# Folding a 2048-point token DFT by even and odd parts, and a small product cut into four column strips

## The chip, the cores and the metric

The kernel runs on 1 core of one Trainium2 chip (the chip has 8). The metric is the device time of one execution in microseconds (us). A run with the hardware profiler shows every instruction of every engine: TensorE (PE, with its weight loads as PEld), VectorE (DVE), ScalarE (ACT), GpSimd (POOL) and SyncE, whose queue SPq issues almost all DMAs here.

## The reference

One layer of a hybrid backbone, on 2048 latent and 256 context tokens of width 1024, in fp32. The parts that the change touches:

```python
mod = silu(c) @ w_ada + b_ada                      # 2 vectors (latent, context), 1024 -> 6144: shift, scale, gate, twice
h   = norm(x) * (1 + scale1) + shift1
z   = h @ w_in                                     # za, zb, q, k, v
def fourier(zb, fw):                               # zb: tokens x 4 groups x 64 channels
    zf = fft2(zb, axes=(tokens, channels), norm='ortho').real
    return einsum('blgc,gcd->blgd', zf, fw)
y = concat(gmlp(za), fourier(zb), attend(q, k, v)) @ w_out
x = affine_ln(ALPHA * x + gate1 * y)
...
x = affine_ln(ALPHA * x + gate2 * conv_ffn(...))
```

The 2-D DFT is done as a channel part (64 points, with `f_w` folded in, in the projection phase) and a token part (2048 points for the latents, 256 for the context, in the Fourier phase). Only the real part is kept.

## The kernel before

It is one program of seven phases, one after another, each a block with a barrier at its end: modulation, projection, Fourier, attention, mix (output projection and norm), FFN up, FFN down. The order on each engine is written by hand, and engines meet at semaphores. Products of high precision are made in three passes of fp32r parts (`PASSES`: high-high, high-low, low-high); ACT rounds a tile to its high part, DVE subtracts for the low part.

**Modulation** (`modulation_phase`). `w_ada` is 1024 x 6144. It is multiplied in chunks of 512 columns (`ADA_COLS`), each with 8 products over k: the stationary side is `silu` (128 x 2), the moving side 128 x 512 of the chunk, and the result takes 2 of the 128 PSUM partitions (L154). Four chunks are made here, eight in the Fourier phase (`ada_product`, L945), where PE has them between pieces of the DFT. Two chunk slots in SBUF; SP loads chunk n when chunk n-2 is done. Between the chunks SP loads `w_in` through a ring of six staging pieces (L114), which ACT rounds (L142) and DVE completes (L165).

**Projection** (`projection_phase`). Nine groups of 256 tokens. `every_group` writes out group 0, runs groups 1 to 6 in a hardware loop of two, and writes out 7 and 8. The channel DFT (`channel_dft`) reads `zbt`, a copy of zb with tokens along the free side, and its rows go to the scratch tensor `chan_dft` (2048+256 tokens x 512: real and imaginary parts of two halves), by `store_ab`.

**Fourier** (`fourier_phase`). The 2048 tokens are split as 4 x 512. For each of four slices i, SP loads 1 MB of `chan_dft` (L791); DVE makes a radix-4 butterfly (L873, L881, L887) and multiplies by twiddles (L897 to L902); ACT rounds (L842) and DVE completes (L909). PE then multiplies with a 512-point table (2 MB, loaded once, L793): 192 instructions of 128x128 weights on 512 columns (`terms`, L954). In between it makes an `ada_product`, and for the cached keys four transposes (`turn_past`, L967). ACT copies results out (L854). The context DFT is 32 instructions at the end (L992). On SP each chunk load is followed by its bias and by the store of an earlier chunk's row, which wait for DVE's sum (L866).

**Mix** (`mix_phase`). 18 tiles of 128 tokens: PE turns a tile of y with eight transposes (`turn_y`, L1639), multiplies with `w_out` in 48 instructions (L1648), and turns the normed tile (L1658). Tiles 2 to 11 run in a hardware loop.

## Time and profile before

| | |
|---|---|
| median of 3 runs | 3102.55 us (3098.46 to 3105.24) |
| the profiled execution | 3104.43 us, span 3102.0 us |
| PE busy | 2874.1 us (93%) |
| DVE busy | 1849.3 us (60%) |
| ACT busy | 1279.6 us (41%) |
| POOL busy | 401.6 us (13%) |
| DMA | 429.97 MB, mean 139 GB/s |
| modulation, projection, Fourier | 0 to 65, 65 to 602, 602 to 739 us |
| attention, mix, FFN | 740 to 1250, 1250 to 1520, 1520 to 3102 us |

Busy times are shares of the span, which is the profiled execution from its first to its last instruction; the run's own time is 2.4 us longer. An engine's busy time says little about a single phase: what matters in a phase is which engine or transfer ends last before its barrier.

### The profile page before, as it was taken

How to read it: one execution, taken by the hardware profiler on the slowest of the kernel's cores; microseconds unless marked ns; L12 is line 12 of the kernel's file. 1: busy time of each engine (PE TensorE's matmuls, PEld its weight loads, DVE VectorE, ACT ScalarE, POOL GpSimd, SP SyncE). 2: the span in 40 equal slices, each digit the busy share in tenths (PEclk: the TensorE clock that was granted, in tenths of full speed). 3: DMA queues.
4: the chain of work that ended last, by engine and by line, in shares of the span. 5: the costliest groups of instructions: out<-in, count | busy, mean ns of one | idle time of the engine just before them, and what ended most of it. 6: DMA issues, size and time to landing. Idle time of an engine off the chain costs nothing. (4 is left out here: it accounts for less than half of the span.)

```text
span 3102.0 us, 51048 instructions
## 1 busy us (share of the span) xinstructions
PE 2874.1 (93%) x17132; PEld 2545.3 (82%) x17132; DVE 1849.3 (60%) x3199; ACT 1279.6 (41%) x2746; POOL 401.6 (13%) x567
## 2 busy tenths in 40 slices
PE   3899999797999999799699999999999979999997
PEld 0899999644887888587599999999999978888875
DVE  4443432262998899477788777666766643443545
ACT  3111111112887888133355565555655532121111
POOL 0000000012222222122400000000000000311312
PEclk8899999898999999899799999999999989999998
DMA  7322222367544560545364555454445435243333
GB/s 251 101 82 92 91 75 74 134 246 199 132 102 89 123 141 16 165 162 185 94 224 166 172 180 185 149 162 149 145 150 163 148 132 169 78 136 117 106 127 131
DMA packets 374228, 429.97 MB, mean 139 GB/s; under 512 B 91911, under 2 KB 270486, under 8 KB 371382
## 3 DMA queue, kind: packets, MB, share of 16 engines
q1 hardware_dynamic: 355353, 418.55, 43.5%
q10 hardware_dynamic: 18720, 9.44, 1.0%
q8 instruction: 88, 1.44, 0.2%
q14 instruction: 67, 0.54, 0.1%
HBM read 305.71 MB, written 124.19 MB: 139 GB/s over the span
## 5 line engine op out<-in xcount | busy, mean ns | idle before, releaser
L1978 PE MATMUL fu_alpha<-fu_h,fu_w 128*128 128x384 f32 x3168 | 577.6, 337 | 19.2 <-DVE fu_h L2204 10.6
L1978 PEld LDWEIGHTS fu_alpha<-fu_h,fu_w 128*128 128x128 f32 x3168 | 556.7, 190 | 21.4 <-issue 21.3
L2464 PE MATMUL fd_acc<-fd_w,fd_f 128*128 128x512 f32 x2376 | 546.2, 392 | 26.5 <-DVE fd_w L2492 17.1
L2464 PEld LDWEIGHTS fd_acc<-fd_w,fd_f 128*128 128x128 f32 x2376 | 447.4, 189 | 125.2 <-issue 17.8
L1978 PE MATMUL fu_beta<-fu_h,fu_w 128*128 128x384 f32 x1584 | 285.4, 334 | 1.2 <-DVE fu_h L2204 1.2
L1978 PEld LDWEIGHTS fu_beta<-fu_h,fu_w 128*128 128x128 f32 x1584 | 275.5, 188 | 1.4 <-issue 1.4
L517 PE MATMUL pj_gps<-pj_ht,w_in 128*128 128x256 f32 x2160 | 268.1, 284 | 0.0
L517 PEld LDWEIGHTS pj_gps<-pj_ht,w_in 128*128 128x128 f32 x2160 | 262.7, 192 | 1.3
L2488 DVE TENSOR_TENSOR fd_f<-fd_f_stage,fd_f 128x512 fp32r<-128x512 f32 (+1 forms) x110 | 91.4, 832 | 284.2 <-ACT fd_f L2444 284.2
L2444 ACT CAST fd_f<-fd_f_stage 128x512 fp32r<-128x512 f32 (+1 forms) x110 | 63.4, 579 | 443.9 <-PE fd_acc L2464 389.3
L2178 DVE TENSOR_TENSOR fu_w<-up_w_stage,fu_w 128x512 fp32r<-128x512 f32 x264 | 181.6, 689 | 85.8 <-ACT fu_w L2042 82.7
L507 PE MATMUL pj_gps<-w_in,pj_ht 128*128 128x512 f32 x912 | 215.7, 394 | 5.3 <-DVE pj_ht L599 5.2
L1648 PE MATMUL mx_acc<-out_w,mx_yt 128*128 128x512 f32 x864 | 208.1, 400 | 0.0
L507 PEld LDWEIGHTS pj_gps<-w_in,pj_ht 128*128 128x128 f32 x912 | 171.1, 189 | 40.9 <-DVE pj_ht L599 5.6
L1282 PE MATMUL at_o_ps<-at_v_parts,at_prob_hi 128*128 128x192 bf16 (+1 forms) x1152 | 195.4, 248 | 1.1 <-DVE at_osum L1350 1.1
L1648 PEld LDWEIGHTS mx_acc<-out_w,mx_yt 128*128 128x128 f32 x864 | 162.7, 190 | 38.2
L2042 ACT CAST fu_w<-fu_w_sums 128x512 fp32r<-128x512 f32 x198 | 122.9, 622 | 164.8 <-PE fu_beta L1978 158.5
L2042 ACT CAST fu_w<-up_w_stage 128x512 fp32r<-128x512 f32 x264 | 163.2, 618 | 61.3 <-PE fu_gamma L1978 56.5
L1282 PE MATMUL at_o_ps<-at_v_parts,at_prob_lo 128*128 128x128 bf16 (+1 forms) x1152 | 186.5, 219 | 0.0
L2178 DVE TENSOR_TENSOR fu_w<-fu_w_sums,fu_w 128x512 fp32r<-128x512 f32 x198 | 136.4, 689 | 53.4 <-ACT fu_w L2042 50.3
L2235 DVE SCALAR_TENSOR_TENSOR fu_result<-fu_g,fu_conv_w,fu_result 128x768 f32<-128x768 f32 (+1 forms) x132 | 134.2, 1016 | 47.2 <-ACT fu_result L2082 46.1
L1978 PE MATMUL fu_gamma<-fu_h,fu_w 128*128 128x384 f32 x792 | 148.4, 335 | 0.0
(194 smaller groups left out, 4294.2 us busy)
## 6 DMA issues: line engine op xcount, KB each, us to landing
up_w_stage<-in_w_gu_dram SPq DMA_DIRECT2D x88, 512.0 KB, 4.2
fu_w_sums<-w_gu_sums SPq DMA_DIRECT2D x132, 256.0 KB, 3.3
fd_w_stage<-in_w_down_dram SPq DMA_DIRECT2D x54, 512.0 KB, 3.6
fd_f_stage<-f_t SPq DMA_DIRECT2D x88, 256.0 KB, 2.7
at_k<-k_t SPq DMA_DIRECT2D x28, 704.0 KB, 12.7
w_gu_sums<-fu_w_sums SPq DMA_DIRECT2D x66, 256.0 KB, 4.9
fo_w<-in_w_ada_dram SPq DMA_DIRECT2D x8, 2048.0 KB, 8.8
up_w_stage<-in_w_gu_dram SPq DMA_DIRECT2D x44, 256.0 KB, 4.6
```

Source lines behind the costliest of these rows:

```text
L507: mm = pe.matmul(out, ht[a][:, s, k, t * P:(t + 1) * P], w[b][:, k, col:col + 512], start=(k, a, b) == (0, HI, HI), stop=(k, a, b) == (KT ...
L517: mm = pe.matmul(out[:, m * G_TOK:(m + 1) * G_TOK], w[a][:, k, col + m * P:col + (m + 1) * P], ht[b][:, s, k, :], start=(k, a, b) == (0, H ...
L1282: mm = pe.matmul(o_ps[:, s, 0:width * HD], part[0:rows, s, b, :], vp[0:rows, parity, v, 0:width, :].rearrange("p n d -> p (n d)"), start=i ...
L1648: mm = pe.matmul(acc[:, s, half * 512:(half + 1) * 512], yt[a][:, s, k, :], w[b][:, k, half * 512:(half + 1) * 512], start=(k, a, b) == (0 ...
L1978: mm = pe.matmul(out, w[x][:, j, k, :], b[y][:, j, k, :], start=opens and (k, x, y) == (0, HI, HI), stop=(k, x, y) == (KH - 1, LO, HI), sk ...
L2042: act.copy(w[HI][:, j], w_source(m, par, j)).then_inc(w_hi, 1)
L2178: dve.tensor_tensor(w[LO][:, j], w_source(m, par, j), w[HI][:, j].bitcast(F32), ALU.subtract).then_inc(w_lo, 1)
L2235: dve.scalar_tensor_tensor(out, grow[:, par, tp:tp + n], par1(cw[:, tp], f), out, ALU.mult, ALU.add).then_inc(tap[tp], 1)
L2444: act.copy(f[HI][:, slot, 0:n], fst[:, slot, 0:n]).then_inc(f_hi, 1)
L2464: mm = pe.matmul(acc[:, t, at], f[a][:, slot, t * P:(t + 1) * P], w[b][:, w_at(st, slot), at], start=is_step(st, 0) and (a, b) == (HI, HI) ...
L2488: dve.tensor_tensor(f[LO][:, slot, 0:n], fst[:, slot, 0:n], f[HI][:, slot, 0:n].bitcast(F32), ALU.subtract).then_inc(f_lo, 1)
```

## The change

**The token DFT is folded.** For a 2048-point DFT of which only the real part is kept, tokens t and 2048-t meet the same cosine and opposite sines, and tokens t and 1024-t the same up to the parity of the output. So DVE adds and subtracts four quarters of the tokens (`fold`), and what is left is four products of 512 tokens with four 512x512 tables (cosine and sine, even and odd outputs). To have token t and its mirrors on one partition, quarters 1 and 3 are stored in reversed order by the projection phase: ACT copies `zbt` with columns reversed for these groups, and `store_ab` writes tiles in reversed order. The bounds of `every_group` must then be numbers, and the hardware loop of groups 1 to 6 is written out. Cosine part and sine part go to separate accumulators; their sum is output k, their difference output 2048-k, for k from 0 to 1023. The first goes to `y`, the second to a new scratch tensor `y_rev` in the order of k, so the mix phase has to turn it over: for tiles 8 to 15 it loads 256 of the 1024 columns from `y_rev` and, in place of two of eight transposes, multiplies with an exchange matrix. Single tokens (0, 512 mirrored, 1024) and output 1024 are treated apart (`e512`, `signs`, `mid`).

**The `w_ada` product is cut in strips.** A chunk of 512 columns becomes four strips of 128 columns, whose products go to columns 0, 32, 64 and 96 of the PE array (`tile_position`) and so to four groups of PSUM partitions. The biases are added by four instructions of 2x128 instead of one of 2x512, in both phases. The Fourier phase has three chunk slots; biases are loaded once and rows stored at its end.

**The order in the Fourier phase is new.** All slices of x, then all four tables (4 MB) are loaded, then the chunks. PE starts after all slices are folded, and the last four `ada_product`s come after the context DFT.

```diff
+def ada_chunk_product(pe, acc, silu, w):
+    for k in range(KT):
+        for q in range(ADA_STRIPS):
+            mm = pe.matmul(acc[ada_strip(q), 0:ADA_STRIP], silu[:, k, :], w[:, k, q * ADA_STRIP:(q + 1) * ADA_STRIP],
+                           start=k == 0, stop=k == KT - 1, tile_position=(0, q * (P // ADA_STRIPS)))
+    return mm
...
-            with eng.Fori(0, (GROUPS - 3) // 2) as i:
-                for s in range(2):
-                    body(i * 2 + (1 + s), 1 - s, True, LAT, False)
+            for g in range(GROUPS - 2):
+                body(g, g % 2, True, LAT, False)
...
+                def load_x(i):
+                    t = i * P
+                    p0 = 1 if i == 0 else 0
+                    sp.dma_start(x[:, i, SET_A, :], chan_dft[t:t + P, :]).then_inc(x_loaded[i], 16)
+                    sp.dma_start(x[p0:P, i, SET_C, :], chan_dft[QUARTER - 1 + t + p0:QUARTER - 1 + t + P, :]).then_inc(x_loaded[i], 16)
+                    if i == 0:
+                        sp.dma_start(x[0:1, i, SET_C, :], chan_dft[HALF_T:HALF_T + 1, :]).then_inc(x_loaded[i], 16)
+                    sp.dma_start(x[p0:P, i, PLUS, :], chan_dft[3 * QUARTER - 1 + t + p0:3 * QUARTER - 1 + t + P, :]).then_inc(x_loaded[i], 16)
+                    sp.dma_start(x[p0:P, i, MINUS, :], chan_dft[HALF_T + t + p0:HALF_T + t + P, :]).then_inc(x_loaded[i], 16)
...
+                fold(0)
+                dve.wait_ge(mid_loaded, 32)
+                dve.tensor_tensor(e512[:, :].rearrange("p (h c) -> p h c", h=2), part(ex[:, 0, :], 0), part(ex[:, 1, :], 0), ALU.add)
...
+                for i in range(1, I):
+                    fold(i)
+                    low_folded(i - 1)
+                low_folded(I - 1)
+                for n in range(4):
+                    dve.wait_ge(table_hi, n + 1)
+                    dve.tensor_tensor(table[LO][:, n], table_raw[:, n], table[HI][:, n].bitcast(F32), ALU.subtract).then_inc(table_lo, 1)
...
+                def transform(m):
...
+                    for n, (tab, side, ri, par) in enumerate(TERMS):
+                        if m == 0:
+                            pe.wait_ge(table_lo, tab + 1)
...
+                        for i in range(I):
+                            for a, b in PASSES:
+                                mm = pe.matmul(o, table[a][:, tab, i, m * P:(m + 1) * P], part(f[b][:, i, side - PLUS, :], ri),
...
                     for k in range(KT):
-                        mm = pe.transpose(yps[:, k, :], yb[:, s, k * P:(k + 1) * P], ident[:, :])
+                        at = slice(k * P, (k + 1) * P)
+                        if mirrored(t) and D_A <= k * P < D_A + D_B:
+                            mm = pe.matmul(yps[:, k, :], yb[:, s, at], exchange[:, :], start=True, stop=True)
+                        else:
+                            mm = pe.transpose(yps[:, k, :], yb[:, s, at], ident[:, :])
```

PE, start of the Fourier phase, before (`fo_kps` are the transposes of cached keys):

```order
L945 MATMUL fo_ada_acc<-fo_w,fo_silu 2x512 x8
L954 MATMUL fo_acc<-fo_ys,fo_table 128x512 x24
L945 MATMUL fo_ada_acc<-fo_w,fo_silu 2x512 x8
L954 MATMUL fo_acc<-fo_ys,fo_table 128x512 x24
L945 MATMUL fo_ada_acc<-fo_w,fo_silu 2x512 x8
```

and PE in the same phase, after (`fo_mid` is output 1024):

```order
L1018 MATMUL fo_acc<-fo_folded,fo_table 128x256 x12
L1024 MATMUL fo_acc<-fo_middle,fo_signs 128x256
L1018 MATMUL fo_acc<-fo_folded,fo_table 128x256 x36
L1033 MATMUL fo_mid<-fo_x,fo_signs 1x256 x4
L1034 MATMUL fo_mid<-fo_middle,fo_signs 1x256
L1003 MATMUL fo_kps<-fo_ident,fo_kc 128x128 x4
L90 MATMUL fo_ada_acc<-fo_w,fo_silu 2x128 x32
```

The chunk product moved from ahead of the first DFT piece to behind it, and has 32 instructions of 128 columns for 8 of 512; a DFT piece has 256 columns for 512.

SP's queue, the first loads of the Fourier phase, before:

```order
L772 DMA fo_cond<-in_conds_dram 128x8x1 x2
L789 DMA fo_tw<-in_twiddle_dram 128x4x8
L791 DMA fo_x<-chan_dft 128x4x512
L793 DMA fo_w<-in_dft_dram 128x8x512
L778 DMA fo_w<-in_w_ada_dram 128x8x512
```

and after:

```order
L840 DMA fo_cond<-in_conds_dram 128x8x1 x2
L791 DMA fo_x<-chan_dft 128x512
L792 DMA fo_x<-chan_dft 127x512
L794 DMA fo_x<-chan_dft 1x512
L795 DMA fo_x<-chan_dft 127x512
L796 DMA fo_x<-chan_dft 127x512
L791 DMA fo_x<-chan_dft 128x512
```

The first slice now comes by five transfers, three of them of 127 rows; the tables and chunks follow behind all four slices.

## Rows read from the trace of the kernel before

**Rows 1.** Windows by stage: us, busy by engine, PE clock, DMA share, GB/s.

```profile
0.00:65.00 65.00, 29.74 (x64) 5.38 (x64) 26.95 (x52) 25.20 (x50) 0.35 (x5) 0.87 0.83 275
600.00:740.00 140.00, 111.30 (x368) 52.40 (x368) 63.19 (x113) 20.36 (x21) 21.99 (x21) 0.90 0.67 234
1250.00:1520.00 270.00, 239.37 (x1144) 197.26 (x1144) 179.21 (x253) 66.76 (x153) 78.72 (x90) 0.94 0.50 164
```

**Rows 2.** Timeline of modulation: start us, us, engine, line, operation, idle before.

```profile
10.43 15.68 PE L154 MATMUL ada_acc<-ada_w,ada_silu 128*2 128x512 f32 x32 [10.43 <-DMA ada_w<-in_w_ada_dram]
...
19.27 0.38 SPq L119 DMA_DIRECT2D ada_w<-in_w_ada_dram  x1
...
27.53 7.03 PE L154 MATMUL ada_acc<-ada_w,ada_silu 128*2 128x512 f32 x16 [1.42 <-DMA ada_w<-in_w_ada_dram]
...
62.61 2.15 DVE L165 TENSOR_TENSOR w_in<-ada_w_in_stage,w_in 128x384 fp32r<-128x384 f32 x4 [0.89 <-ACT w_in L142]
```

**Rows 3.** Windows of full and of idle DMA, columns as in the first group.

```profile
8.00:10.00 2.00, 0.00 (x0) 0.00 (x0) 0.00 (x0) 0.00 (x0) 0.00 (x0) 1.00 1.05 397
18.00:20.00 2.00, 2.00 (x6) 0.40 (x5) 2.00 (x5) 1.42 (x4) 0.00 (x0) 1.00 0.03 9
```

**Rows 4.** Timeline of PE in the Fourier phase.

```profile
620.21 9.41 PE L945 MATMUL fo_ada_acc<-fo_w,fo_silu 128*2 128x512 f32 x16 [21.29 <-DMA fo_w<-in_w_ada_dram]
629.55 5.85 PE L954 MATMUL fo_acc<-fo_ys,fo_table 128*128 128x512 f32 x24
...
692.95 7.03 PE L945 MATMUL fo_ada_acc<-fo_w,fo_silu 128*2 128x512 f32 x16
699.90 0.66 PE L967 MATMUL fo_kps<-fo_ident,fo_kc 128*128 128x128 f32 x4
...
732.24 3.73 PE L992 MATMUL fo_acc<-fo_x 128*128 128x128 f32 x32
```

**Rows 5.** Timeline, start of the Fourier phase: first x load, first butterflies, second butterflies.

```profile
603.86 0.51 SPq L791 DMA_DIRECT2D fo_x<-chan_dft  x1
...
609.16 2.50 DVE L873 TENSOR_TENSOR fo_sums<-fo_x 128x512 f32<-128x512 f32 x4 [18.01 <-DMA fo_x<-chan_dft]
...
626.68 5.23 DVE L873 TENSOR_TENSOR fo_sums<-fo_x 128x512 f32<-128x512 f32 x4
```

**Rows 6.** Groups by line and shape: count, busy us, mean ns of one.

```profile
L517 PE MATMUL pj_gps<-pj_ht,w_in 128*128 128x256 f32 x2160 | 268.1, 284 | 0.0
...
L1361 DVE TENSOR_TENSOR out_w<-out_w_stage,out_w 128x1024 f32 x6 | 7.3, 1216 | 0.0
...
L909 DVE TENSOR_TENSOR fo_ys<-fo_y,fo_ys 128x2048 fp32r<-128x2048 f32 x4 | 9.6, 2394 | 6.1 <-ACT fo_ys L842 6.1
...
L842 ACT CAST fo_ys<-fo_y 128x2048 fp32r<-128x2048 f32 x4 | 7.6, 1893 | 44.1 <-DVE fo_y L902 44.1
...
L1426 ACT CAST out_w<-out_w_stage 128x1024 f32 x6 | 6.3, 1049 | 0.0
...
L881 DVE TENSOR_TENSOR fo_y<-fo_sums 128x256 f32<-128x256 f32 x16 | 5.7, 420 | 0.1
```

**Rows 7.** DMA issues of 600 to 740 us: count, KB, median us to landing.

```profile
fo_w<-in_w_ada_dram SPq DMA_DIRECT2D x8, 2048.0 KB, 8.8
```

**Rows 8.** Timeline, end of the Fourier phase: SP's first DMA of attention.

```profile
739.95 0.34 SPq L1111 DMA_DIRECT2D at_ident<-in_ident_dram  x1
```

**Rows 9.** Timeline of PE in attention: two instructions, one of 128 columns between them.

```profile
1235.04 0.25 PE L1282 MATMUL at_o_ps<-at_v_parts,at_prob_hi 128*128 128x192 bf16 x1
...
1235.18 0.25 PE L1282 MATMUL at_o_ps<-at_v_parts,at_prob_hi 128*128 128x192 bf16 x1
```

**Rows 10.** Timeline of PE in the mix phase, one tile.

```profile
1396.74 1.03 PE L1658 MATMUL mx_hps<-mx_ident,mx_xn 128*128 128x128 f32 x8
1397.61 1.04 PE L1639 MATMUL mx_yps<-mx_ident,mx_y 128*128 128x128 f32 x8
1398.40 11.44 PE L1648 MATMUL mx_acc<-out_w,mx_yt 128*128 128x512 f32 x48
```

More of the change, by code:

```diff
@@ L129, in _ @@
                     load_w_in(k)
-                sp.wait_ge(acc_read, N)
-                sp.dma_start(mod[:, 0:2 * D], row[:, :, :].rearrange("v n c -> v (n c)")).then_inc(stored, 16)
-                sp.wait_ge(stored, 16)
+                sp.wait_ge(acc_read, N * ADA_STRIPS)
+                for v in range(2):
+                    sp.dma_start(mod[v, 0:2 * D].rearrange("(n q c) -> q n c", q=ADA_STRIPS, c=ADA_STRIP), ada_rows(row, v)).then_inc(stored, 16)
+                sp.wait_ge(stored, 32)
                 sp.wait_ge(rpb_stored, 48)
@@ L172, in _ @@
                     dve.wait_ge(acc_done, n + 1)
-                    dve.tensor_tensor(row[:, n, :], acc[0:2, n], bias[:, n, :], ALU.add).then_inc(acc_read, 1)
+                    for q in range(ADA_STRIPS):
+                        at = ada_strip(q)
+                        dve.tensor_tensor(row[at, n, :], acc[at, n, 0:ADA_STRIP], bias[at, n, :], ALU.add).then_inc(acc_read, 1)
                 for k in (KT - 2, KT - 1):
@@ L434, in group @@
                     act.wait_ge(ab_done, g * NT + NT)
-                    act.copy(zbt[:, :, :].rearrange("p m t -> p (m t)"), gps[:, n, :]).then_inc(slot_read[n], 1)
+                    columns = gps[:, n, :].rearrange("p (m t q) -> p (m t) q", m=2, t=NT)
+                    if reversed_from(g, 0) is not None:
+                        columns = columns[:, :, P - 1::-1]
+                    act.copy(zbt[:, :, :].rearrange("p m (t q) -> p (m t) q", q=P), columns).then_inc(slot_read[n], 1)
                     gelu(1)
@@ L810, in _ @@
+                load_past(0)
+                for c in range(SLOTS):
+                    load_chunk(c)
+                    if c == 0:
+                        load_biases()
+                for m in range(I):
+                    if m == 1:
+                        sp.wait_ge(f_lo, I)
+                        sp.wait_ge(patched, 1)
                         sp.dma_start(ctab, dft256_in.rearrange("r (i p) m -> p r i m", p=P)).then_inc(xc_loaded, 16)
+                        sp.wait_ge(mid_done, 1)
@@ L843, in _ @@
[L843 to L856 removed]
+                flat = lambda ap: ap.rearrange("p s c -> p (s c)")
@@ new lines, in _, with copy_past @@
+                for i in range(I):
+                    act.wait_ge(folded, 2 * i + 2)
+                    if i == 0:
+                        act.wait_ge(patched, 1)
+                    act.copy(flat(f[HI][:, i]), flat(x[:, i, PLUS:MINUS + 1, :])).then_inc(f_hi, 1)
+                for n in range(4):
+                    act.wait_ge(table_loaded[n], 16)
+                    act.copy(flat(table[HI][:, n]), flat(table_raw[:, n])).then_inc(table_hi, 1)
+                def copy_past(t):
+                    act.wait_ge(kc_turned, t + 1)
+                    if t:
+                        act.wait_ge(kc_stored, t * 32)
+                    act.copy(kct[HI][:, :, :].bitcast(F32R), kps[:, :, :]).then_inc(kc_hi, 1)
@@ new lines, in _ @@
+                for m in range(I):
+                    act.wait_ge(acc_done, m + 1)
+                    if m >= 2:
+                        act.wait_ge(acc_read, 2 * m - 2)
+                    act.copy(even[:, m % 2, :], acc[:, m % 2, 0, :]).then_inc(even_copied, 1)
+                    if m == 0:
+                        act.wait_ge(mid_done, 1)
+                        act.copy(mid_out[:, :], mid[0:1, :]).then_inc(mid_copied, 1)
+                    copy_past(m)
+                for t in range(2):
+                    act.wait_ge(ctx_done, t + 1)
+                    act.copy(ctx_out[:, t, :], acc[:, t, 0, 0:256]).then_inc(ctx_copied, 1)
@@ new lines, in _ @@
+                for m in range(I):
+                    s = m % 2
+                    dve.wait_ge(even_copied, m + 1)
+                    if m >= 2:
+                        dve.wait_ge(stored[s], 16 * 2)
+                    dve.tensor_tensor(out[:, s, 0, :], acc[:, s, 1, :], even[:, s, :], ALU.add).then_inc(acc_read, 1)
+                    dve.tensor_tensor(out[:, s, 1, :], even[:, s, :], acc[:, s, 1, :], ALU.subtract).then_inc(acc_read, 1)
+                    low_past(m)
+                    add_bias(m)
@@ new lines, in _ @@
+                for m in range(I):
+                    if m == 0:
+                        pe.wait_ge(f_lo, I)
+                    transform(m)
+                    if m == 0:
+                        for i in range(I):
+                            pe.matmul(mid[0:1, :], signs[:, P:P + 1], part(x[:, i, PLUS, :], 0), start=i == 0, stop=False)
+                        pe.matmul(mid[0:1, :], signs[0:1, P:P + 1], e512[:, :], start=False, stop=True).then_inc(mid_done, 1)
+                    turn_past(m)
+                    ada_product(m)
@@ L1544, in mix_phase, with y_uses @@
         use = lambda t, s: (t - s) * 8
+        FIRST_MIRRORED, N_LOOPED = T_LAT // 2 // P, 6
+        mirrored = lambda t: isinstance(t, int) and FIRST_MIRRORED <= t < N_LAT
+        def y_uses(t, s):
+            if not isinstance(t, int):
+                return use(t, s) + 16
+            return sum(48 if mirrored(n) else 16 for n in range(s, t + 1, 2))
         def every_tile(body, first_span_done=lambda: None):
@@ L1549, in loop @@
                 body(1, 1, LAT)
-                with eng.Fori(0, (LATE - 2) // 2) as i:
+                with eng.Fori(0, (N_LOOPED - 2) // 2) as i:
                     for s in range(2):
                         body(i * 2 + (2 + s), s, LAT)
+                for t in range(N_LOOPED, LATE):
+                    body(t, t % 2, LAT)
                 first_span_done()
```

394 lines of the change are left out of this document (177 added, 217 removed).

## The prediction

> **What bounds the kernel now.** I read the windows by stage first [rows 1], since each phase ends at a barrier and the shares of the whole span mix phases with different limits. Three phases are touched in a way that can move time. In modulation PE is busy for less than half and the DMA engines for 83%: transfers and the staging ring end it, DVE's last low part ending at 62.61 + 2.15 = 64.8 us [rows 2]. In the mix phase PE is the bound (239 of 270 us). In the Fourier phase PE is busy 111 of 140 us, all of it after 620: from there its timeline has hardly a gap [rows 4]. PE's first work there waits 21.29 us for its first chunk, so the phase is a start of 18 us (602 to 620) in which only transfers and DVE run, and then 115.8 us of PE, to 732.24 + 3.73 = 736.0. Attention's first DMA is issued at 739.95 [rows 8], so 4.0 us pass between. The projection is left alone: writing out its loop changes no work of PE, and I cost that at nothing; its cover is PE's own queue of long products, and a lost overlap would show as PE gaps at group bounds.
>
> **PE's work in the Fourier phase.** Before: 8 pieces of 24 instructions, each 5.85 us, 46.8 in all; 8 chunk products of 7.03, 56.2; four sets of transposes of 0.66, 2.6; the context DFT 3.7 [rows 4]. Sum 109. After, 192 instructions have 256 columns for 512. The projection's instructions of this shape cost 268.1 / 2160 = 0.124 us each [rows 6], so a transform of 48 takes 5.95; with the small product of `signs` (two passes of 256 columns on fp32; 16 passes of 512 columns take 7.03, so 0.22 each) it is 6.4. Four make 25.6 for 46.8. The new output 1024 needs 10 such passes, 2.1. A halving of the DFT is thus worth about 19 us of PE, if PE is the bound.
>
> **The chunk product in strips.** The row has 16 instructions for 8 products, so an fp32 product is two passes, one after the other on the same weights' place; a pass of 512 columns takes 0.44 us, so one of 128 takes 0.107 to 0.117 (the context DFT: 3.73 / 32 = 0.117 [rows 4]). A chunk now has 32 products, 64 passes. No row shows strips, so the cost is bounded from both sides. One after another: 64 x 0.117 = 7.5 us, no better than 7.03. Four at a time: 16 x 0.107 = 1.7, say 1.9. The two passes of a product follow each other and go to the same strip, so the second must wait for the first, and, if PE keeps its order, only the second pass of one product overlaps the first of the next. That is 32 x 0.107 = 3.4, and I take 3.6. The issue of instructions doesn't forbid it: two instructions with their weights pass in 1235.18 - 1235.04 = 0.14 us [rows 9], 0.07 each, which would give 4.5 at most.
>
> The Trainium skill, "TensorE: Matmul & The Clock Gate", Part 3 on packing, reports three column tiles at 2.38 times the speed. The same part says that a weight load overlaps running products only where the row group differs, which strips of columns don't fulfil; by that every load of 2 columns would stand in line and a chunk would cost 7.5 us or more. No row here decides between them.
>
> **The start of the phase.** This is the step on which the forecast turns. Before, the first slice of 1 MB is issued at 603.86 and DVE starts on it at 609.16 [rows 5]. Loads flow at 397 GB/s [rows 3], or 2.62 us for 1 MB, and 1/16 of that, 24.8 GB/s, for one of 16 DMA engines. The first slice now has three transfers of 127 rows of 2 KB. 127 is a prime: it can't be cut into equal shares for several engines. All other large transfers have 128 or 64 rows, or like numbers. So two ends: spread as before, the slice lands at 609.1; or each of the three goes whole through one engine, and the same one, 0.26 MB each at 24.8 GB/s, 10.5 us, 31.5 for three less the 2.0 of a spread, so the slice lands at 638.6. I take the second, since all that is behind in the same queue then also waits for that engine's share.
>
> The Trainium skill, "DMA: Bandwidth & Descriptors", section "Why a DMA increments its semaphore by 16 and not by 1", states that a hardware-queued copy uses the largest number of engines up to 16 that divides both sides' slowest dimension, and names 127 partitions as a case of one engine. The trace has no such transfer.
>
> From there: slices 1 to 3 follow at 2.62 us, 646.5; the two single rows behind them (DVE waits for them before `fold(1)`) 646.6; four tables, 657. DVE: four instructions of 128x256 (5.7 / 16 = 0.36 each [rows 6]) and two of 128x512 (2.50 / 4 = 0.62 [rows 5]) make a fold of 2.7; the patch 0.7; low parts of 128x1024 1.2 each (L1361). 646.6 + 0.7 + 3 x 2.7 + 3 x 1.2 = 659; the last low part ends at 660.2. ACT rounds the last slice (1.05, L1426) after the last fold, then tables at 1.9 each (L842), just ahead of DVE, which needs 2.2 for each of four (L909, 2.39 with its end): 660.6 + 8.8 = 669.4. PE may take the last quarter of transform 0 only then: 12 x 0.124 = 1.5 us, twice that at the lower clock, which is what it gets after idling: the phase's first 16 passes took 9.41 us for the later 7.03 [rows 4]. DVE beside POOL can also slow down (5.23 for 2.50 [rows 5]). Together 673, three to four more if POOL's steps on the cached values fall badly, two less if not. Before, PE had started at 620; 53 us of idle replace its work.
>
> **Remaining PE work.** From 673: output 1024 2.1, four sets of transposes 2.7, three transforms 19.2, context 3.7, eight chunks at 3.6 = 28.8. Sum 56.5: 729.5. A second chain runs beside it: there are three slots, so chunk 7 is loaded when chunk 4 is multiplied, which comes after the context DFT: 673 + 2.1 + 0.7 + 3.6 + 3 x (6.4 + 0.7 + 3.6) + 3.7 + 3.6 = 718.8. A chunk lands 8.8 us after issue (median, queues with others [rows 7]); alone I take 8.0, then 3.6 of product: 730.4. This ends last. SP's other waits (for POOL's steps, for stores) are done some us before. Then DVE's four small sums, two stores of `mod` (issue and landing, all in all 1.3 us more than the 4.0 of before): attention's first DMA at 730.4 + 5.3 = 735.7, against 739.95: 4.2 us gained. What is late next, if the chunks get cheaper, is this chain of loads, then DVE's start.
>
> **Modulation.** The first 16 passes keep the next load back till 19.27 [rows 2], and DMA is idle from 18 to 20 [rows 3]. With the product at 3.6, plus 2 at the lower clock, SP issues at 16: the idle stretch is filled, and the later waits of PE (1.42 before 27.53) tell that loads are the bound. I take 3.0 us. The 16 small sums of 2x128 in place of four of 2x512 cost DVE more: no row has the shape; at least 0 and at most 0.36 each (128x256), say 0.2, so 3.2 for 2.5, on the way of the ring's last pieces: 0.7 lost. Net 2.3 gained. The second store of `mod` and the biases of four rows lie beside the ring's end.
>
> **Mix.** For eight tiles two transposes become products of two passes, two passes more of 0.117 on PE's path [rows 10]: 8 x 0.23 = 1.9 lost. Two more DMAs per tile on SP (0.3 to 0.5 each) hide behind the 13.1 us of PE per tile (1398.40 + 11.44 less 1396.74). The reversed read of `zbt` has one read for one.
>
> **The sum:** 4.2 + 2.3 - 1.9 = 4.6 us. The profiled execution has 3104.4, 1.9 over the median, so 3099.8 by it and **3098 us** as a median. From no change a measurement of this kernel tells about 0.2%, 6.2 us: the forecast is within.
>
> **Rivals.**
> Strips don't overlap (slower): a chunk costs 7.5, the eight make 59.7, PE ends at 673 + 27.7 + 59.7 = 760.4 and attention starts at 765.7, 25.8 later; modulation loses its 0.7 and mix 1.9: 28.4 lost, 3131. It decides from about 4.3 us a chunk, where 673 + 27.7 + 8 x 4.3 + 5.3 = 740.4 eats up the phase's gain and mix that of modulation. For it: same row groups, two passes for fp32, which no row shows in strips. Against: weights load beside running products everywhere in this trace (PEld busy 52 of 140 us beside PE [rows 1]).
> Strips overlap fully: 1.9 a chunk. The chain of loads then ends at 673 + 2.8 + 1.9 + 3 x 9.0 + 3.7 + 1.9 + 8.0 + 1.9 = 720.2, attention at 725.5: 14.4 + 2.3 - 1.9 = 14.8 gained, 3088. Against it: the two passes.
> The 127 rows are spread, strips as in the forecast: everything from 638.6 on is 29.5 us earlier, 34 gained, 3068. For it: nothing in the trace forbids uneven shares. Both together, spread and strips that don't overlap: 28.4 - 29.5, no change, 3101.
> Writing out the loop costs time (instructions fetched while PE works): would show in the projection alone; the written out groups 7 and 8 and the Fourier phase show no such gaps [rows 4], and I give it no case of its own.
>
> **Chances.** Forecast 0.42, strips in turn 0.23, full overlap 0.15, rows spread 0.12, spread with strips in turn 0.08. The forecast's own range is 3090 to 3107 (a chunk from 3.0 to 4.5, the start 4 us either way), and a third of it lies beyond 6.2 us of gain. So faster: 0.14 + 0.14 + 0.12 + 0.02 = 0.42; slower: 0.04 + 0.22 + 0.01 = 0.27; same 0.31. The range leaves out the spread case and reaches to strips in turn with its start a little later: 3080 to 3134.
>
> **What would show it.** In the profile after: DVE's first fold at about 639 and a stretch of some 30 us with DMA share near 1/16 (forecast), or at 609 (spread). A chunk's 64 passes in 3.6 us, in 7.5, or in 1.9. PE's last chunk product waiting for its load (chain of loads) or not. The last table low part at 669. The mix phase longer by 2 us, the projection as long as before. The forecast is wrong if strips cost over 4.3 us, or if the first slice lands early; also if SP, held by the ring of one engine, issues the chunk loads late.

## The result, and the profile after

The changed kernel takes **3117.4 us** (median; 3116.3 to 3119.8) where the kernel before takes 3102.0: a ratio of 1.0053, 95% interval 1.0038 to 1.0067. It is slower by about 15 us; the forecast was 3098. The measured time is inside the stated range, but on the other side of the kernel before. The profiled execution has a span of 3117.6 us for 3102.0, so the two traces account for 15.6 us.

Where they part is seen by placing the stage marks side by side. Attention's first DMA is the end of the Fourier phase:

```profile
756.36 0.34 SPq L1163 DMA_DIRECT2D at_ident<-in_ident_dram  x1
```

That is 16.4 us later than in [rows 8]. The mix phase, from its first product to the end of its last, takes 245.6 us for 244.2, 1.4 more. The FFN phases, which the change doesn't touch, take 2.2 us less; 16.4 + 1.4 - 2.2 = 15.6. In modulation and projection together 1.5 us were already lost: the Fourier phase's first DMA is at 603.63 for 602.17. So 14.9 of the 15.6 us are lost within the Fourier phase. Against the forecast (4.6 us gained) the spans are off by 20.2 us: 19.1 in the Fourier phase, 3.8 in modulation and projection (2.3 forecast as a gain, 1.5 lost), less 0.5 in mix and 2.2 in the FFN. These are two single executions: in runs 8 and 9 below, whose Fourier phase has the same code as here, it lasts 151.3 and 150.8 us for 152.7.

The phase in one row, columns as in [rows 1]: TensorE busy 59.66 us for 111.30, its clock 0.68 for 0.90, and the DMA engines no busier than before:

```profile
600.00:740.00 140.00, 59.66 (x693) 48.65 (x695) 42.45 (x70) 19.25 (x22) 23.95 (x21) 0.68 0.68 234
```

**Its start.** SP's queue, timeline of the kernel after (start, duration of the issue, line, transfer). Some of the issues themselves take 5 to 10 us:

```profile
604.70 0.57 SPq L791 DMA_DIRECT2D fo_x<-chan_dft  x1
605.32 0.30 SPq L792 DMA_DIRECT2D fo_x<-chan_dft  x1
605.66 4.64 SPq L794 DMA_DIRECT2D fo_x<-chan_dft  x1
610.35 0.28 SPq L795 DMA_DIRECT2D fo_x<-chan_dft  x1
610.66 9.73 SPq L796 DMA_DIRECT2D fo_x<-chan_dft  x1
620.44 10.09 SPq L791 DMA_DIRECT2D fo_x<-chan_dft  x1
```

Windows of the same kernel (columns as in [rows 1]):

```profile
608.00:612.00 4.00, 0.00 (x0) 0.00 (x0) 0.00 (x0) 0.00 (x0) 0.00 (x0) 0.50 0.06 24
616.00:620.00 4.00, 0.00 (x0) 0.00 (x0) 0.00 (x0) 0.00 (x0) 0.00 (x0) 0.50 0.07 26
```

A DMA share of 0.06 is 1/16 of the 16 DMA engines' time: it is as if one engine worked, at 24 to 26 GB/s, and the others stood still, and so do TensorE, VectorE, ScalarE and GpSimd. SP hands out nothing new meanwhile: its issues of 9.73 and 10.09 us fill this stretch. VectorE's timeline shows the consequence:

```profile
641.20 1.43 DVE L932 TENSOR_TENSOR fo_x<-fo_x 128x256 f32<-128x256 f32 x4 [48.59 <-DMA fo_x<-chan_dft]
...
649.18 0.41 DVE L947 TENSOR_TENSOR fo_middle<-fo_even 1x256 f32<-1x256 f32 x1 [5.22 <-DMA fo_even<-chan_dft]
...
663.11 11.67 DVE L956 TENSOR_TENSOR fo_table<-fo_table_raw,fo_table 128x2048 fp32r<-128x2048 f32 x4 [0.58 <-ACT fo_table L894]
```

The first fold stands at 641.2 where the first butterfly of before stood at 609.16 [rows 5]. The line at 649.18 waits for the two single rows, which are queued behind all four slices.

**Its rounds.** TensorE's timeline, rounds 0 and 1 and the tail. A round is a transform, the transposes of a tile of cached keys and a chunk product. L1018 is a transform, L1003 the four transposes of cached keys, L90 a chunk product in strips:

```profile
666.54 2.90 PE L1018 MATMUL fo_acc<-fo_folded,fo_table 128*128 128x256 f32 x12 [66.15 <-DVE fo_table L956]
...
679.20 0.66 PE L1003 MATMUL fo_kps<-fo_ident,fo_kc 128*128 128x128 f32 x4
679.79 1.93 PE L90 MATMUL fo_ada_acc<-fo_w,fo_silu 128*2 128x128 f32 x64
681.65 1.70 PE L1018 MATMUL fo_acc<-fo_folded,fo_table 128*128 128x256 f32 x12
683.27 0.69 PE L1024 MATMUL fo_acc<-fo_middle,fo_signs 1*128 1x256 f32 x2
683.90 4.58 PE L1018 MATMUL fo_acc<-fo_folded,fo_table 128*128 128x256 f32 x36
692.61 1.12 PE L1003 MATMUL fo_kps<-fo_ident,fo_kc 128*128 128x128 f32 x4 [4.13 <-DMA fo_kc<-in_cache_k_dram]
693.66 3.60 PE L90 MATMUL fo_ada_acc<-fo_w,fo_silu 128*2 128x128 f32 x64
...
727.92 4.51 PE L1042 MATMUL fo_acc<-fo_x 128*128 128x128 f32 x32
732.36 3.67 PE L90 MATMUL fo_ada_acc<-fo_w,fo_silu 128*2 128x128 f32 x128
...
747.35 3.59 PE L90 MATMUL fo_ada_acc<-fo_w,fo_silu 128*2 128x128 f32 x64 [6.17 <-DMA fo_w<-in_w_ada_dram]
```

Three things are to be seen. A chunk's 64 passes take **1.93 us** for the 7.03 of [rows 4]. In every later round the transposes wait some 4 us (4.13, 4.14, 3.68) for a load of keys that [rows 4] shows no wait for. And after each wait the same 64 passes take 3.1 to 3.6 us. The window at that place says why (PE clock is the third number from the right):

```profile
688.00:692.00 4.00, 0.48 (x5) 0.27 (x3) 1.28 (x2) 0.58 (x1) 0.00 (x0) 0.98 1.01 353
692.00:696.00 4.00, 3.39 (x52) 2.36 (x56) 0.48 (x1) 0.58 (x1) 0.17 (x1) 0.50 1.10 380
```

TensorE was granted 0.98 of 2.4 GHz in the first of the two, in which it stood idle but for 0.48 us, and 0.50 of it, the 1.2 GHz level, in the second. What it had waited for was queued on SP behind a chunk:

```profile
659.49 22.66 SPq L818 DMA_DIRECT2D fo_w<-in_w_ada_dram  x2
682.19 0.67 SPq L835 DMA_DIRECT2D y_mixed<-fo_out  x1
...
683.64 0.51 SPq L801 DMA_DIRECT2D fo_kc<-in_cache_k_dram  x1
```

The 22.66 us cover SP's wait for the slot; the chunk's 2 MB are handed out at its end, and the keys, 256 KB, follow 1.5 us later and land at 692.6, 9.0 us after their issue. What TensorE has to do in these 9 us is the rest of one transform: it is done at 688.48, 4.8 us after the issue. In the kernel before the same load was issued here (SP's queue in its timeline):

```profile
688.47 0.36 SPq L752 DMA_DIRECT2D fo_kc<-in_cache_k_dram  x1
```

and it was needed at 699.90 [rows 4], 11.4 us later, since a piece of the DFT and a whole chunk product of 7.03 us lay between. In the new order the transposes come ahead of the round's chunk product and no longer behind it, while the chunk load, and with it the keys behind it, still waits for the product before to end.

### The profile page after: what moved, and what is told of

It reads as the page before. It is cut to its first block and busy times, and to the rows that moved or that the text cites. A ratio compares the mean times of both kernels' runs of the same rounds, so it can differ in the third digit from the quotient of the medians.

```text
span 3117.6 us, 51637 instructions
## 1 busy us (share of the span) xinstructions
PE 2814.5 (90%) x17742; PEld 2548.9 (82%) x17742; DVE 1831.6 (59%) x3176; ACT 1278.0 (41%) x2746; POOL 403.7 (13%) x568
## 5 line engine op out<-in xcount | busy, mean ns | idle before, releaser
L552 PE MATMUL pj_gps<-pj_ht,w_in 128*128 128x256 f32 x2160 | 268.1, 284 | 0.0
L1727 PE MATMUL mx_acc<-out_w,mx_yt 128*128 128x512 f32 x864 | 210.7, 403 | 0.0
L1727 PEld LDWEIGHTS mx_acc<-out_w,mx_yt 128*128 128x128 f32 x864 | 164.6, 192 | 38.9
```

The source lines that it names most:

```text
L552: mm = pe.matmul(out[:, m * G_TOK:(m + 1) * G_TOK], w[a][:, k, col + m * P:col + (m + 1) * P], ht[b][:, s, k, :], start=(k, a, b) == (0, H ...
L1727: mm = pe.matmul(acc[:, s, half * 512:(half + 1) * 512], yt[a][:, s, k, :], w[b][:, k, half * 512:(half + 1) * 512], start=(k, a, b) == (0 ...
```

## The experiments

Medians are compared with that of the kernel after, 3117.4 us, and the ratios with the kernel before, run on the same chip at the same time.

**1. The three transfers of 127 rows, spread.** The kernel after with

```
+ for lo, hi in (((1, 113), (113, P)) if p0 else ((0, P),)):
+     sp.dma_start(x[lo:hi, i, which, :], chan_dft[off + lo:off + hi, :]).then_inc(x_loaded[i], 16)
...
- dve.wait_ge(x_loaded[i], 80 if i == 0 else 64)
+ dve.wait_ge(x_loaded[i], 128 if i == 0 else 64)
```

> Change to the kernel after: each of the three transfers of 127 rows of the first slice is cut into 112 and 15 rows; nothing else. Theory (127 rows go through one DMA engine, three times 10.5 us, and this holds the whole start of the Fourier phase back): DVE's first fold starts at about 611 instead of 641.2, all that follows moves by the same 29.5 us, attention's first DMA from 756.4 to 727, median 3117.4 - 29.5 = 3088 us (3084 to 3092). Rival (once the rows are spread, the transfers behind them, 4 MB of tables and 6 MB of chunks, or DVE with POOL beside it set PE's start): the fold starts early, PE's first transform starts at 645 or later, under 22 us gained, over 3096 us.

Measured: 3091.4 us, 26.0 gained; ratio 0.9963 [0.9949, 0.9977]. VectorE's first fold in the timeline of this run, and then the window of 608 to 612:

```profile
611.86 1.43 DVE L936 TENSOR_TENSOR fo_x<-fo_x 128x256 f32<-128x256 f32 x4 [19.41 <-DMA fo_x<-chan_dft]
```

```profile
608.00:612.00 4.00, 0.00 (x0) 0.00 (x0) 0.14 (x1) 0.00 (x0) 0.00 (x0) 0.50 0.86 255
```

The fold starts 29.3 us earlier, and attention 27.7 (728.65). The same bytes in the same queue, only cut otherwise: the theory holds, and this one edit turns the change from slower into faster than the kernel before.

**2. Only one of the three spread.** The second quarter's transfer is cut, two stay whole (the wait is for 96).

> Change to the kernel after: one of the three transfers of 127 rows (the second quarter's) is cut into 112 and 15 rows, two stay whole. Theory (each whole transfer of 260 KB costs its 10.5 us on one DMA engine, one after the other): DVE's first fold starts at about 631 (641.2 less 10), a third of the gain of the run with all three cut, attention's first DMA at about 746, median 3108 us (3105 to 3111). Rival (what holds the start back is SP, which waits for room in the queue of one engine, whichever transfer comes last; the first two would cost nothing by themselves): under 4 us or over 18 us gained.

Measured: 3107.9 us, 9.4 gained; ratio 1.0027 [1.0018, 1.0037]. The first fold is at 630.72, 10.5 us earlier than in the kernel after, and attention's first DMA at 743.96. The dose is right: one whole transfer costs 10.5 us, and three cost 29.3 (run 1), so they go one after another.

**3. The keys ahead of the chunk.** The kernel after with

```
 for m in range(I):
     ...
+    if m < PAST_TILES - 1:
+        load_past_keys(m + 1)
     load_chunk(SLOTS + m)
     store_rows(m)
-    if m < PAST_TILES - 1:
-        load_past(m + 1)
+    if m < PAST_TILES - 1:
+        load_past_values(m + 1)
     store_past(m)
```

> Change to the kernel after: in each of the first three rounds SP issues the load of the next cached keys ahead of the chunk load instead of behind it and behind the store of the rows. Theory (PE's transposes wait 4.13, 4.14 and 3.68 us for keys that queue behind 2 MB, and the clock that falls then makes the next chunk product 3.1 to 3.6 us for 1.93): the three waits are gone, the rounds take 11 to 12 us for 15 to 16, 12 to 15 us gained, attention's first DMA at 742 to 744, median 3103 us (3100 to 3106). Rival (the chain of chunk loads through three slots sets the end whatever PE does in between): the waits move to the chunks' loads, under 5 us gained, 3112 us or more.

Measured: 3108.5 us, 8.9 gained; ratio 1.0022 [1.0012, 1.0032]; attention's first DMA at 745.39, 11.0 us earlier. That lies between the two expectations. TensorE's timeline of this run shows both parts:

```profile
687.99 0.60 PE L1008 MATMUL fo_kps<-fo_ident,fo_kc 128*128 128x128 f32 x4
688.51 1.93 PE L90 MATMUL fo_ada_acc<-fo_w,fo_silu 128*2 128x128 f32 x64
...
720.98 1.93 PE L90 MATMUL fo_ada_acc<-fo_w,fo_silu 128*2 128x128 f32 x64 [3.00 <-DVE fo_bias L928]
727.77 3.59 PE L90 MATMUL fo_ada_acc<-fo_w,fo_silu 128*2 128x128 f32 x64 [4.86 <-DMA fo_w<-in_w_ada_dram]
736.78 3.19 PE L90 MATMUL fo_ada_acc<-fo_w,fo_silu 128*2 128x128 f32 x64 [5.42 <-DMA fo_w<-in_w_ada_dram]
```

The rounds shrink to 9.1, 11.4 and 10.5 us, with the product at 1.93 in each; one wait for keys, of 2.15 us, is left in the second of them. But the last three products, which had waited 7.1 us for loads, now wait 10.3, and 3.0 for VectorE's sums. The theory was right on the wait, and the rival right that the chain of chunk loads takes back a part.

**4. Both edits together.**

> The edits of the two kernels before it in one: rows of the first slice cut into 112 and 15, and the keys' load ahead of the chunk load. Theory (the two causes are independent: a start that is 29.5 us late, and waits inside the rounds behind a chunk load): the gains add up, 26.0 and 8.9 us by the medians, attention's first DMA at 717.7 (756.36 less 27.7 less 11.0), median 3082.5 us (3078 to 3087). Rival (with the start early, GpSimd's 11.5 us for each tile of cached values, which begins only when the values land, keeps SP from the next chunk load and takes over): rounds of 12 us or more for 9 to 11, attention's first DMA at 722 or later, median 3087 us or more.

Measured: 3080.0 us; ratio 0.9936 [0.9921, 0.9951]; attention's first DMA at 716.29. The gains of runs 1 and 3 add up to 34.9, and together they give 37.4, so neither cause hides the other. GpSimd's 11.5 us in this and two later expectations was a misreading of mine: its five instructions on a tile take 4.4 us from first to last when VectorE isn't busy beside them (0.62, 1.16, 0.61, 1.16, 0.61); the rest was waiting.

**5. Strips alone, on the kernel before.** `ada_chunk_product` and its rows of four partitions in both phases; nothing else of the change.

> Change to the kernel before: the w_ada product in four strips in modulation and in the Fourier phase, as the change has it, and no folding, no exchange matrix, no reversed rows. Theory (strips are worth 5.1 us a chunk at full clock, but in the first half of the phase DVE's 15 us a slice bound the before, so only chunk products 4 to 7 come off the path): PE's last product ends at about 715 for 736, attention's first DMA at 719 for 739.95, 18 to 21 us gained, median 3083 us (3079 to 3087). Rival (chunk loads or the load of the keys become the new wait, PE falls to the lower clock and the strips give their gain back, as in the kernel after): under 8 us gained, 3094 us or more.

Measured: 3101.9 us, ratio 0.9994 [0.9985, 1.0004]: nothing gained, as the rival said. A product costs 1.93 us for 7.03, 5.1 less, eight times, yet attention starts at 741.74, 1.8 us later than in [rows 8]. TensorE's timeline of this run:

```profile
685.58 1.93 PE L90 MATMUL fo_ada_acc<-fo_w,fo_silu 128*2 128x128 f32 x64
...
703.74 1.11 PE L993 MATMUL fo_kps<-fo_ident,fo_kc 128*128 128x128 f32 x4 [8.21 <-DMA fo_kc<-in_cache_k_dram]
...
727.26 3.74 PE L1018 MATMUL fo_acc<-fo_x 128*128 128x128 f32 x32
```

GpSimd's last tile of values, and SP's store of it, in the same timeline:

```profile
730.40 0.62 POOL L959 CAST fo_vparts<-fo_vc 128x512 bf16<-128x512 f32 x1 [7.57 <-DMA v_parts<-fo_vparts]
```

```profile
734.86 0.34 SPq L788 DMA_DIRECT2D v_parts<-fo_vparts  x1
```

TensorE ends 5 us before its old end, at 731.0, after 8.2 us of waiting for keys; then SP waits for GpSimd, which had itself waited for the store of the tile before it. In the first half VectorE's slice sets the pace (a wait of 6.2 to 6.7 us on its parts in each of three rounds), and the pieces of the DFT behind these waits take 7.2 to 8.4 us for 5.85. The long product was a cover for all these.

**6. The same with SP's order mended.** Values of tile 1 are asked for, and those of tile 0 stored, in round 5 already, and keys go ahead of chunks 6 and 7:

```
+ if c >= CHUNKS - 2:
+     load_keys(c - CHUNKS + 3)
  load_chunk(c)
  ...
  if c >= CHUNKS - 2:
+     store_keys(c - CHUNKS + 2)
+     load_values(c - CHUNKS + 4)
+     store_values(c - CHUNKS + 3)
  if c == 5:
+     load_values(1)
+     store_values(0)
```

> Change to the kernel before: strips as in the earlier run, plus the order of SP's DMAs on the cached keys and values: values of tile 1 asked for in round 5 already, keys ahead of the chunk load in rounds 6 and 7. Theory (strips alone gave nothing since the wait for the keys, 8.2 us, and the chain of GpSimd's 11.5 us a tile of values that begins at 695 took the place of PE's work): PE's wait of 8.21 us is gone, the last store of values is issued at about 722 for 734.9, attention's first DMA at 727 to 731 for 741.7, 10 to 14 us gained on the run with strips alone, median 3090 us (3086 to 3094). Rival (VectorE, whose slices take 15 to 16 us in the first half, and the chunk loads bound it anyway): under 5 us gained, 3097 us or more.

Measured: 3089.5 us, ratio 0.9965 [0.9953, 0.9977]; the last store of values is issued at 722.77, attention's first DMA at 731.46, half a microsecond later than expected. So strips with this order are 11 us faster than the kernel before, and with the old order none. The new order without strips wasn't tried, so how the 11 divide stays open. The wait for the keys didn't vanish as I had said: 4.78 us of it are left; the gain came from it and from GpSimd's earlier chain.

**7. The folding without strips.** The kernel after with products of 512 columns. The Fourier biases lie on two partitions, in folded rows no longer read, and are loaded later.

> Change to the kernel after: the w_ada product in one piece of 512 columns again, in both phases (biases and rows of the Fourier phase lie on two partitions in place of folded rows no longer read, and their load comes after output 1024). Theory (a chunk costs 7.0 us for 1.9 to 3.6, and the waits for the keys stay, since the keys are issued with the chunk load): each of the four rounds 4 to 5 us longer, the last four chunks end at about 778 for 751, attention's first DMA at about 783, 27 us lost, median 3144 us (3138 to 3150). Rival (the strips' gain is already hidden by the waits for loads): under 8 us lost, 3125 us or less.

Measured: 3149.9 us; ratio 1.0148 [1.0131, 1.0165]; attention's first DMA at 783.36. TensorE's timeline of this run, where L89 is the product in one piece:

```profile
680.01 7.03 PE L89 MATMUL fo_ada_acc<-fo_w,fo_silu 128*2 128x512 f32 x16
...
698.86 1.12 PE L999 MATMUL fo_kps<-fo_ident,fo_kc 128*128 128x128 f32 x4 [5.06 <-DMA fo_kc<-in_cache_k_dram]
...
751.46 27.63 PE L89 MATMUL fo_ada_acc<-fo_w,fo_silu 128*2 128x512 f32 x64
```

The phase ends 27.0 us later, as expected, the whole kernel is 32.5 us longer by the medians; of the 5.5 between, 3.8 are the FFN's first part, which has a shorter and a longer length without a change in it (see the last section). The waits for keys are there in this kernel too (5.06, 4.23, 3.69), in rounds of 19 to 20 us. So they come neither from the strips nor from the length of the round, but from the order: the keys are asked for only when the chunk product is over and its slot is loaded again, and then TensorE has one transform, 6.8 us, before it needs them.

**8. One sum for sixteen, in modulation alone.**

```
+ pool.memset(bias[:, :, :], 0.0).then_inc(cleared, 1)
...
+ dve.memset(acc[:, :, 0:ADA_STRIP], 0.0).then_inc(cleared, 1)
...
- for n in range(N):
-     dve.wait_ge(acc_done, n + 1)
-     for q in range(ADA_STRIPS):
-         dve.tensor_tensor(row[at, n, :], acc[at, n, 0:ADA_STRIP], bias[at, n, :], ALU.add)
+ dve.wait_ge(acc_done, N)
+ at = slice(0, (ADA_STRIPS - 1) * (P // ADA_STRIPS) + 2)
+ dve.tensor_tensor(row[at, :, :], acc[at, :, 0:ADA_STRIP], bias[at, :, :], ALU.add)
```

> Change to the kernel after, in modulation alone: bias and accumulators are cleared first, and one VectorE instruction over partitions 0 to 97 adds all four chunks, for 16 instructions of 2 partitions. Theory (the 16 sums take 5.05 us in the ring of the last pieces, and give back what the earlier loads had gained): the sum takes 0.7 us, the last low part ends at 61.5 to 62.7 instead of 64.91, projection's first DMA at 61.8 to 63.0 instead of 65.21, 2.2 to 3.4 us gained, median 3114.6 us. Rival (the last pieces' transfers end the phase whatever VectorE does, and the sums are beside them): under 0.8 us gained.

Measured: 3114.4 us, 3.0 gained; ratio 1.0045 [1.0031, 1.0058]. VectorE's timeline in the kernel after, and then in this one:

```profile
52.01 5.05 DVE L198 TENSOR_TENSOR ada_row<-ada_acc,ada_bias 2x128 f32<-2x128 f32 x16
...
62.83 2.08 DVE L188 TENSOR_TENSOR w_in<-ada_w_in_stage,w_in 128x384 fp32r<-128x384 f32 x4 [0.90 <-ACT w_in L167]
```

```profile
52.23 0.68 DVE L202 TENSOR_TENSOR ada_row<-ada_acc,ada_bias 98x512 f32<-98x512 f32 x1
...
58.68 2.30 DVE L194 TENSOR_TENSOR w_in<-ada_w_in_stage,w_in 128x384 fp32r<-128x384 f32 x4 [1.00 <-ACT w_in L170]
```

The last low part ends at 61.0 for 64.9 and the projection's first DMA is at 61.28 for 65.21. The sums lie on the path one for one: 4.4 us fewer give 3.9.

**9. Transposes for the exchange matrix, in mix.** The mirrored tiles' pieces are turned with `ident` in place of `exchange`, and so stay in reverse order.

> Change to the kernel after, in the mix phase alone: the mirrored tiles' two pieces are transposed with the identity, as the other pieces are, in place of the products with the exchange matrix; their rows stay in reverse order, so these tiles' part of the output is not the reference's. Theory (a product of two passes for a transpose costs 0.24 us a tile on PE's path, eight tiles): a mirrored tile's period 12.94 for 13.18 us, the phase 1.9 us shorter, median 3115.5 us (3114 to 3117). Rival (the difference lies beside other work, or the reversed rows' load with its one wait of 3.8 us makes the phase's loss): tile period unchanged, under 0.7 us gained, and the wait of 3.8 us still there.

Measured: 3119.5 us, ratio 1.0060 [1.0046, 1.0073]; no gain in the whole, but the phase shows one. Tiles of the kernel after, then of this one (L1727 is the tile's product):

```profile
1387.58 0.61 PE L1716 MATMUL mx_yps<-mx_exchange,mx_y 128*128 128x128 f32 x4
1388.03 0.60 PE L1718 MATMUL mx_yps<-mx_ident,mx_y 128*128 128x128 f32 x4
1388.38 11.46 PE L1727 MATMUL mx_acc<-out_w,mx_yt 128*128 128x512 f32 x48
...
1401.57 11.46 PE L1727 MATMUL mx_acc<-out_w,mx_yt 128*128 128x512 f32 x48
```

```profile
1384.73 11.44 PE L1727 MATMUL mx_acc<-out_w,mx_yt 128*128 128x512 f32 x48
...
1397.67 11.44 PE L1727 MATMUL mx_acc<-out_w,mx_yt 128*128 128x512 f32 x48
```

A mirrored tile's period is 13.19 us with the exchange matrix and 12.94 without (13.18 and 12.94 at other tiles). The phase, first product to last, is 3.2 us shorter in this execution, of which 8 x 0.24 = 1.9 are the tiles. That total alone would show nothing: in the eight executions here with the changed mix code, first to last start of a product take 243.2 to 245.6 us, in the three with the old code 241.7 to 243.8. In the same execution the FFN's parts, the same code, are 3.7 and 2.3 us longer, and all ahead of the mix phase, also the same code, 3.1 us shorter. So the price of 1.9 us is shown in the tiles and not in the total; that the medians differ by 2.1 us the other way I can't explain beyond such lengths. The wait of 3.81 us for reversed rows is in both executions, so it isn't the exchange matrix's.

**10. Rows spread and the products a round earlier.** Rows cut as in run 1; the two single rows loaded ahead of the slices; chunk product 0 inside transform 0, before its last table, and each later product one round earlier; one sum over partitions 0 to 97 in both phases. The expectation says that keys then go ahead of chunks. The edit doesn't do that: run 3's order isn't in it, and SP still issues a round's chunk load before its keys.

> Change to the kernel after: rows of the first slice cut into 112 and 15; the two single rows loaded ahead of the slices; chunk product 0 done inside transform 0, while PE waits for the last table, and each later product with it one round earlier, so that keys go ahead of chunks; one sum per chunk over partitions 0 to 97 in both phases. Theory (what bounds the start is a row of waits, 5.9 us of it for the single rows; what bounds the end is the chain of loads through three slots, 6 us; and the keys' waits cost 9): DVE's table parts end at about 640, the last product at about 700, attention's first DMA at 704 to 709, modulation 2.5 us shorter, median 3066 us (3061 to 3072). Rival (GpSimd's chain on the cached values, 11.5 us a tile, or DMA itself bounds from there): attention's first DMA at 714 or later, median over 3076 us.

Measured: **3067.8 us**, ratio 0.9894 [0.9879, 0.9909], 33 us under the kernel before of the same session. Attention's first DMA is at 701.80, 2.2 us ahead of the lower end of what I expected. Two waits for keys are left, 2.87 and 2.64 us; the first in TensorE's timeline (the product behind it takes 3.50 us):

```profile
652.89 0.66 PE L1016 MATMUL fo_kps<-fo_ident,fo_kc 128*128 128x128 f32 x4 [2.87 <-DMA fo_kc<-in_cache_k_dram]
```

Its windows (columns as in [rows 1]) tell what is likely to bound it now:

```profile
610.00:620.00 10.00, 0.00 (x0) 0.00 (x0) 9.49 (x21) 3.14 (x3) 0.00 (x0) 0.50 1.04 390
...
640.00:650.00 10.00, 10.00 (x122) 8.24 (x120) 1.31 (x3) 0.95 (x2) 0.00 (x0) 1.00 1.05 387
...
680.00:690.00 10.00, 7.68 (x146) 6.76 (x149) 0.94 (x4) 0.74 (x2) 4.16 (x5) 0.89 1.02 363
```

From 610 to 690 the DMA engines are at full share in every window of 10 us, at 346 to 393 GB/s, where the kernel before had 0.67 over the phase [rows 1]. The half of the rival that named DMA fits this, though the time it gave was too long; no run takes bytes away to test it. How the 33 us divide among the edits is open.

## Why the prediction failed, step by step

Attention's first DMA was forecast at 735.7, counted from an unchanged start of the phase, and came at 756.4. These 20.7 us are to be accounted for. In short: the step that failed is the waits in the rounds, put at nothing; they cost 12 of the 20.7 us.

- **The start: right.** The second of the two ends, one DMA engine for all 127 rows, is what happened (638.6 forecast, 641.2 measured; 1.5 of the difference is the later start of the phase). By the Trainium skill, "DMA: Bandwidth & Descriptors", section "Why a DMA increments its semaphore by 16 and not by 1", 127 rows go through one engine; the trace agrees, with a share of 0.06 and 24 to 26 GB/s, and run 2 with 10.5 us a transfer. Transform 0 ends at 676.9 for 673: 3.9 us late, with the 1.5 in it. The term that was short is the table's low parts, 2.9 us each for 2.2. GpSimd works on the cached values from 661.78 to 672.6 beside them; in run 10 the two parts that end before GpSimd starts take 2.29 and 2.28 us, and the last, beside it, 2.70. The forecast had named that case, with three to four us more.
- **The rounds: the failed step.** "SP's other waits (for POOL's steps, for stores) are done some us before." True of those two but for 0.7 us of SP's stores (in the sum below); it passed over what TensorE waits for itself: the keys, issued behind the chunk. From 676.9 to the end of the context DFT 55.5 us pass for 42.2 forecast, 13.3 more. The three waits are 11.95 of it. The other 1.4 are a balance: transforms of 6.8 us for 6.4, and transposes, a transform and the context DFT at the lower clock, less what the strips saved. Rows 4 showed the transposes with no wait, but 11.4 us after their keys' issue. I kept the wait at nothing although the new order puts only a transform between issue and use, and didn't ask whether a load that takes 9 us from its issue still hides behind it. Run 3 shows the mechanism, run 7 that it doesn't depend on strips or on the round's length, run 5 that the kernel before has it as soon as its products, which lay between issue and use, are shorter.
- **The strips: mechanism wrong, and sized from that.** "The second must wait for the first" gave 3.6 us. It is 1.93 at full clock: 64 passes take the time of 16 (16 x 0.117 = 1.9), so the four strips run beside each other throughout, and no second pass that waits for its first holds up the other strips. Where 3.6 stands in the trace it is the clock, so the forecast's number was met in three of eight chunks, for a reason that it did not have. The case "strips in turn", with the largest chance beside the forecast, is out. The rule of the Trainium skill, "TensorE: Matmul & The Clock Gate", Part 3, that a weight load overlaps only where the row group differs, would by the prediction's estimate give 7.5 us or more. The trace contradicts it: four strips of one row group take 1.93 us for 64 passes, 30 ns each. By "strips overlap fully" the time would have been 3088, and this too was wrong, since its chain had no wait for keys.
- **The chain of loads: right as a chain, mis-sized.** The last product does wait for its load, as said. But chunk 7 lands 12.5 us after its issue (734.87 to 747.35), not 8.0: chunk 6 was issued 7 us ahead of it and keys' and values' stores between them. 4.5 us more. From the last product to attention's DMA 5.4 us pass for 5.3 forecast.
- The sum: 3.9 + 13.3 + 4.5, plus 0.7 for the issue of chunk 7's load, which stands behind SP's stores of keys and values, less 1.8 for product 4 (1.83 for 3.6), plus 0.1 at the end = 20.7.
- **Modulation: a gain of 2.3 forecast, none measured.** The loads came earlier and the stages with them (VectorE's sums start at 52.01 for 54.41), as the forecast has it. But a sum of 2x128 costs 0.32 us and not 0.2: 5.05 for 2.47, 2.6 more where 0.7 had been set aside. Run 8 gives it back. The bound was right (at most 0.36), the value in it was not: one of 2x512 takes 0.62, one of 2x128 with a quarter of the elements half of that, and the number of partitions makes no difference (98x128 takes 0.28 in run 10).
- **Mix: right.** 0.24 us a tile for 0.23. One wait of 3.81 us is now for reversed rows, but in the kernel before the same tile waited 4.74 us for its rows of y, so it is no new cost. **Projection: right as far as shown.** Its products are unchanged, 268.1 us for 2160 instructions as in [rows 6]; from its first DMA to that of the Fourier phase pass 538.4 us for 537.1, but in runs 5 and 6, which keep the hardware loop, 538.9 and 538.0.

The halved transforms themselves did what the forecast said: TensorE is busy 59.7 us up to 740, and 4.8 more to the end of the phase, for 111.3 [rows 1]. Some 47 us of work less, and a phase that ends 16 us later: 63 us of new idle time. Of these 46 lie ahead of the first product (666.5 for 620.2 [rows 4]), nearly all others are waits for loads.

## What to carry to other kernels

Before cutting an engine's work, list every transfer that this work has been hiding, with its time from issue to landing and what stands ahead of it in its queue: once the work between its issue and its use is shorter than that, the order of the queue sets the time, and a small load behind a 2 MB one costs a wait and then the clock (here 4 us, and 3.1 to 3.6 us for 1.93). Look at the row count of every DMA that a new indexing makes; a shift by one row can turn 128 into 127, and here a cut into 112 and 15 mended it. And price a saving by undoing it on both sides: the same strips were worth nothing on one kernel and 27 us of the Fourier phase on another, depending on what else was in the way.

## What the runs showed of the hardware

- An fp32 product with two columns of weights runs at four strips at once: 64 passes of 128 columns in 1.93 us, against 7.03 for 16 passes of 512 (3.6 times as long), both at full clock; at the 1.2 GHz level it takes 3.59 us.
- Three transfers of 127 rows (260 KB each) went at the rate of one DMA engine, 24 to 26 GB/s, 10.5 us each. They don't only come late. They hold the queue's owner too: SP's issues took 4.64, 9.73 and 10.09 us, and all that stood behind them in that queue waited, transfers of 128 rows too.
- One VectorE instruction over 98 partitions and 512 elements in each takes 0.68 us where sixteen of 2x128 take 5.05; over 98x128 it takes 0.28. The price is to clear the rows between the strips once: 0.48 us on VectorE and 0.53 on GpSimd in run 8, while the first chunk is still being loaded.
- The FFN's first part, unchanged in all twelve kernels, took 973.7 to 973.8 us from the first to the last start of its first products (`fu_alpha`) in five of the profiled executions and 977.2 to 977.7 in six (975.4 in one). I don't know what decides between them. It makes a difference of 3.7 us in a total hard to tell from an effect, and is why stage times stand beside medians above.
